# Norm stages of a two-block transformer kernel: token tile 1 starts ahead of tile 0's last held weight, turns and weight splits in a new order

## The reference

```python
def rmsnorm(x, w):
    xf = x.astype(jnp.float32)
    y = xf * lax.rsqrt(jnp.mean(xf * xf, axis=-1, keepdims=True) + RMS_EPS)
    return (y * w.astype(jnp.float32)).astype(x.dtype)

# first block, behind the mixers
x = x + merged @ w_merge_out                       # merge stage, norm with ffn_norm
x = x + (silu(h @ w_gate) * (h @ w_up)) @ w_down   # first feed-forward, norm with norm_mix_w_2
# second block
x = x + nsa_mixer(h, ...)                          # NSA-output stage, norm with norm_cross_w_2
x = x + memory_cross_attention(h, mem_n, ...)      # cross-output stage, norm with norm_ffn_w_2
x = x + conv_ffn(h, ...)                           # second feed-forward, norm with final_norm_w_2
return rmsnorm(x, final_norm_w)
```

## Time and profile before

| | us |
|---|---|
| median of 3 runs | 1783.47 |
| lowest and highest run | 1782.94, 1786.35 |
| profiled execution | 1786.1 |
| its span | 1784.3 |
| TensorE busy in it | 1720.2 (96%) |
| VectorE, ScalarE, GpSimd busy | 955.8, 844.5, 960.9 |

### The profile page before, as it was taken

How to read it: one execution, slowest core, us unless ns; L and a number is a source line. 1 busy time by engine, 2 the same in 40 slices (tenths; PEclk the granted TensorE clock), 3 DMA queues, 4 the chain that set the end, 5 groups by cost and what they waited for, 6 DMA issues and landing times. The chain is left out here.

```text
span 1784.3 us, 27614 instructions
## 1 busy us (share of the span) xinstructions
PE 1720.2 (96%) x10430; PEld 1526.1 (86%) x10430; DVE 955.8 (54%) x1628; ACT 844.5 (47%) x1681; POOL 960.9 (54%) x701
## 2 busy tenths in 40 slices
PE   6999999999999999999989999999899999999998
PEld 4898887888879998999868978888788789989996
DVE  2246564444538851674138469984224388518842
ACT  3234454232336641554336358874434466426642
POOL 2353332334445774776336459982652368648852
PEclk8999999999999999999989999999999999999999
DMA  6332221223342333233325330002442223323331
GB/s 222 93 83 57 72 69 45 60 64 91 117 165 70 97 125 100 78 113 124 89 76 145 109 87 10 14 24 71 135 128 69 67 81 101 118 84 95 118 120 47
DMA packets 222900, 162.09 MB, mean 91 GB/s; under 512 B 9768, under 2 KB 197296, under 8 KB 222768
## 3 DMA queue, kind: packets, MB, share of 16 engines
q1 hardware_dynamic: 221712, 159.26, 29.7%
q10 hardware_dynamic: 1056, 1.06, 0.2%
HBM read 156.09 MB, written 2.11 MB: 89 GB/s over the span
## 5 line engine op out<-in xcount | busy, mean ns | idle before, releaser
L352 POOL TENSOR_TENSOR w_low<-ring,w_high 128x1024 fp32r<-128x1024 f32 (+2 forms) x223 | 484.6, 2177 | 604.4 <-ACT w_high L344 604.0
L365 PE MATMUL psum<-hT,w_high 128*128 128x512 f32 (+1 forms) x1104 | 379.7, 344 | 7.4 <-PEq L184 6.1
L344 ACT ACTIVATE w_high<-ring 128x1024 fp32r<-128x1024 f32 (+2 forms) x223 | 212.3, 955 | 361.1 <-PE psum L367 356.5
L367 PE MATMUL psum<-hT,w_low 128*128 128x512 f32 (+1 forms) x1104 | 373.9, 339 | 0.0
L366 PE MATMUL psum<-hL,w_high 128*128 128x512 f32 (+1 forms) x1104 | 373.9, 339 | 0.0
L365 PEld LDWEIGHTS psum<-hT,w_high 128*128 128x128 f32 x1104 | 210.9, 191 | 28.9 <-issue 7.3
L367 PEld LDWEIGHTS psum<-hT,w_low 128*128 128x128 f32 x1104 | 210.7, 191 | 22.8
L366 PEld LDWEIGHTS psum<-hL,w_high 128*128 128x128 f32 x1104 | 211.0, 191 | 20.0
L1799 POOL TENSOR_TENSOR w_low<-ffn_sums,w_high 128x512 fp32r<-128x512 f32 x120 | 169.8, 1429 | 49.7 <-ACT w_high L1794 49.4
L365 PE MATMUL psum<-ffn_th,w_high 128*128 128x256 f32 x640 | 181.7, 284 | 4.7 <-DVE ffn_g L2047 3.1
L1799 POOL TENSOR_TENSOR w_low<-ring,w_high 128x512 fp32r<-128x512 f32 x120 | 155.7, 1300 | 55.6 <-ACT w_high L1794 49.1
(11 more groups left out here) (441 smaller groups left out, 3760.1 us busy)
## 6 DMA issues: line engine op xcount, KB each, us to landing
ring<-in_w_in SPq DMA_DIRECT2D x58, 512.0 KB, 3.6
ring<-in_ffn_w_up SPq DMA_DIRECT2D x44, 512.0 KB, 3.8
ring<-in_w_gate SPq DMA_DIRECT2D x22, 512.0 KB, 3.8
ring<-in_w_up SPq DMA_DIRECT2D x22, 512.0 KB, 4.9
ring<-in_w_down SPq DMA_DIRECT2D x20, 512.0 KB, 3.9
ring<-in_ffn_w_down SPq DMA_DIRECT2D x20, 512.0 KB, 3.8
ring<-in_nsa_w_in SPq DMA_DIRECT2D x18, 512.0 KB, 3.6
ring<-in_ca_wkv SPq DMA_DIRECT2D x16, 512.0 KB, 3.7
```

Of the source, the lines that this page charges most:

```text
L344: nc.scalar.activation(tile_view(w_high, n, SPLIT), tile_view(ring, n, RING), ACT.Copy).then_inc(w_hi, 1)
L352: nc.gpsimd.tensor_tensor(tile_view(w_low, n, SPLIT), tile_view(ring, n, RING), tile_view(w_high, n, SPLIT), ALU.subtract).then_inc(w_lo, 1)
L365: nc.tensor.matmul(ps, lhsT=sh, rhs=mh, start=first, stop=False)
L367: return nc.tensor.matmul(ps, lhsT=sl, rhs=mh, start=False, stop=last)
```

## The change

On TensorE (`held_tile(t, i)` is held weight i of token tile t) the order of the held part becomes (0,0) (0,1) (1,0) (0,2) (1,1) (1,2), then for token tiles 2 and 3: the first held weight, the turn of the tile two before, the other two held weights; then turn 2 and, with `last_turn`, turn 3. In the key stage turn 3 stands ahead of tile 1. On ScalarE a Sqrt of the constant `eps` into an unused column of `stat` (L679 of the changed kernel) stands ahead of the first chunk's squares, the last held split goes ahead of the memory's high parts, and the next stage's first weights are split ahead of the high parts of tiles 1 and 2, the third one ahead of tile 3's in nsaO alone. The stages with `whole` (merge, cross output) keep their order of splits and high parts.

```diff
+                        def held_tile(t, i):
+                            s = per - held + i
+                            wh, wl = tile_for(pe, n0 + s, wname)
+                            for kk in range(plan[n0 + s][2]):
+                                mm = products(s, kk, wh, wl, t)
+                            if t == tiles - 1:
+                                mm.then_inc(w_used, 1)
+                            elif i == held - 1:
                                 mm.then_inc(tile_done, 1)
-                            if t >= 1 and not store:
-                                if t == 1:
-                                    pe.wait_ge(out_v, tiles)
-                                    if between is not None:
-                                        between["turn"](pe)
-                                norm.turn(pe, t - 1)
-                        if held and not store and last_turn:
-                            norm.turn(pe, tiles - 1)
+
+                        def turn_tile(t):
+                            if store:
+                                return
+                            if t == 0:
+                                pe.wait_ge(out_v, tiles)
+                                if between is not None:
+                                    between["turn"](pe)
+                            norm.turn(pe, t)
+
+                        if held:
+                            held_tile(0, 0)
+                            held_tile(0, 1)
+                            held_tile(1, 0)
+                            held_tile(0, 2)
+                            held_tile(1, 1)
+                            held_tile(1, 2)
+                            for t in range(2, tiles):
+                                held_tile(t, 0)
+                                turn_tile(t - 2)
+                                held_tile(t, 1)
+                                held_tile(t, 2)
+                            turn_tile(tiles - 2)
+                            if last_turn:
+                                turn_tile(tiles - 1)
...
                         split_high(a, n0 + SPLIT)
+                        nc.scalar.activation(stat[:, 151:152], eps, ACT.Sqrt)
                         for t in range(tiles):
                             a.wait_ge(out_v, t + 1)
                             norm.square(a, t, 0, BANK)
+                        split_high(a, n0 + per)
                         if between is not None:
                             between["a"](a)
-                        split_high(a, n0 + per)
                         for t in range(tiles):
                             a.wait_ge(out_v, tiles + t + 1)
                             norm.square(a, t, BANK, BANK)
                             norm.root(a, t)
-                            if whole is not None and t == tiles - 2:
-                                split_high(a, n0 + per - min(SPLIT, per) + SPLIT + 1)
+                            if not store and t >= tiles - 2:
+                                split_high(a, n0 + per - min(SPLIT, per) + SPLIT + 1 + (t == tiles - 1))
                             if t >= 1 and not store:
                                 norm.high_part(a, t - 1)
-                            if t == tiles - 2:
-                                split_high(a, n0 + per - min(SPLIT, per) + SPLIT + (2 if whole is not None else 1))
-                        split_high(a, n0 + per - min(SPLIT, per) + SPLIT + 2)
+                            if whole is not None and t == tiles - 2:
+                                split_high(a, n0 + per - min(SPLIT, per) + SPLIT + 2)
                         if not store:
+                            if not last_turn and whole is None:
+                                split_high(a, n0 + per - min(SPLIT, per) + SPLIT + 3)
                             norm.high_part(a, tiles - 1)
...
         def last_norm_turn(pe, i):
 
-            if i == 2:
+            if i == 1:
                 norm2.turn(pe, NT - 1)
```

More of the change, by code:

```diff
@@ L600, in _ @@
                             between["pe"](pe)
-                        for t in range(tiles if held else 0):
-                            for s in range(per - held, per):
-                                wh, wl = tile_for(pe, n0 + s, wname)
-                                for kk in range(plan[n0 + s][2]):
-                                    mm = products(s, kk, wh, wl, t)
-                                if t == tiles - 1:
-                                    mm.then_inc(w_used, 1)
-                            if t < tiles - 1:
-                                mm.then_inc(tile_done, 1)
-                            if t >= 1 and not store:
-                                if t == 1:
-                                    pe.wait_ge(out_v, tiles)
-                                    if between is not None:
-                                        between["turn"](pe)
-                                norm.turn(pe, t - 1)
```

## The result

The changed kernel takes 1769.91 us (median of 4 runs, 1768.38 to 1771.35), the kernel before, run beside it, 1783.40 (1782.94 to 1786.35): a ratio of 0.9921, with a 95% interval of 0.9904 to 0.9938. That is 13.5 us less; 1769.7 was forecast. The profiled execution after took 1771.35, with a span of 1769.6 us at a mean granted clock of 0.992; before it was 1786.1, 1784.3 and 0.986. The two mean clocks can't be set against one another: from 26.99 to 31.68 the products of 512 columns start 0.43 apart in the profile after, as they do at 1.2 GHz, and 0.23 further on, yet a window from 15 to 35 says 1.00 there; before, where the same stretch is as slow, it says 0.74.

What follows compares the result with a forecast made beforehand. TensorE's waits for w_low, the low weight half GpSimd makes (11.3 us in 8 waits), were taken as the bound a norm-stage change can touch. -1.9 - 1.9 - 10.2 + 0.2 = -13.8, from 1783.5 to 1769.7; range 1765.5 to 1776.

Steps and rivals of the forecast that it cites:

- Merge stage: Merge stage: wait for the third weight's low half gone, next weight split earlier; next stage starts 1.9 us earlier.
- The cover of 1.52 for the added 1.48: Merge stage, ScalarE: early table load (1.28) and root (0.2) hidden by the 1.52 us in which ScalarE waited.
- Cross-output stage: Cross-output stage: same stage and waits as merge, 1.9 us less; the following 1.93 wait for VectorE keeps its size.
- rival (b): Merge and cross-output gains given back at the head of the feed-forward stages; price up to 3.8 us, chance 0.10.
- NSA-output and key stage: NSA-output and key stages: key tile 3 begins 10.2 us earlier, from holes 7.5, restarts and a turn 0.7, clock 2.0.
- the wait left for the first two key weights: Key stage, TensorE: tile 0 without a wait listed, tile 1's weight about 0.5 us late.
- The 2.0 us given for it: Key stage: 22 products at 1.2 GHz took 4.6 us where 2.6 would do; 2.0 of the 10.2.
- the split ahead of the memory parts: NSA-output stage: last held weight split before the memory high parts; alone removes the 1.55 us wait, reordering alone leaves little.
- Feed-forward output stages: Two feed-forward output stages: tile 0 comes 1.36 us later, table load of 1.28 goes; +0.08 each, sum +0.2.
- Rival (a): Clock falls all the same; 1.2 GHz stretches elsewhere may come out longer or shorter; price 2 to 4 us, chance 0.12.
- Rival (c): Key stage keeps most waits, its second and third weight tiles late for another reason; price up to 10 us, chance 0.08.
- (d): Key stage: a late ring tile load holds up normalised tiles and key tile 4; 1784 to 1790 us, chance 0.03.

Runs made afterwards that it cites:

- early-split versions: Two versions of the changed kernel with tile 0's held pieces together in the feed-forward output stages and next-stage weights split earlier: 1772.64 and 1770.88 us.
- last-turn experiment: The kernel before with one edit, the NSA norm's last turn ahead of key tile 1 and not tile 2: 1776.13 us, ratio 0.9951.
- last turn and splits: The kernel before with the last turn ahead of key tile 1 and the changed split order, without held order or early root: 1775.18 us, 0.9941.
- last turn back: The changed kernel with the last turn ahead of key tile 2, as before: 1773.15 us, ratio 0.9927.
- the three loads: The changed kernel with two more table loads beside the early root, ahead of the first chunk's squares: 1775.76 us, ratio 0.9952.
- all next splits earlier: Changed kernel, tile 0 together in feed-forward outputs; second and third next weights split earlier in NSA-output and first feed-forward output stages: 1772.64 us, 0.9927.
- the second key split early: Changed kernel, tile 0 together in feed-forward outputs; in the NSA-output stage the second key weight split ahead of tile 3's square: 1770.88 us, 0.9923.
- the third split in the feed-forward too: Changed kernel, tile 0 together in feed-forward outputs; third weight split ahead of the last high part in the first feed-forward output too: 1766.84 us, 0.9901.

## Why the prediction was right, step by step

The total came out 0.2 from the forecast. Part of that is luck: the stages gave 13.3 where 13.8 was forecast, and the difference between the medians also holds what the clock does elsewhere.

- **Merge stage, 1.9 forecast, 1.83 measured.** The cover of 1.52 for the added 1.48 held to 0.03. The experiment without the root and the one without the held order confirm the two halves: neither half reaches more than 0.6 alone. Turn 0 and turn 1 found their data, and the next stage begins in a wait of 0.22 for the weight instead of 0.2 for tile 1's low part.
- **Cross-output stage, 1.9 forecast, 1.85 measured.** And the wait at the head of the second feed-forward kept its size, 1.93: rival (b) did not come. The reason given, that VectorE's work there runs on from the last low part, holds as far as the size of that wait shows.
- **NSA-output and key stage, 10.2 forecast, 9.66 measured.** The holes went where the steps put them. The term that was off is the wait left for the first two key weights: 0.23 and 0.77, where the text had none and about 0.5, which is 0.5 of the 0.54. GpSimd's subtraction for key tile 0 at 1245.88 was counted at 2.4 and took 2.87 beside VectorE's scaling; the one for tile 1 at 1250.63 began during a scaling too. The forecast named no rival for that, although the trace before had such a meeting (below); it is the same contention that undid the two early-split versions. The clock of 1.00 came as forecast, and the last-turn experiment shows that the low stretch goes with the hole of 4.20. The 2.0 us given for it is not measured apart from the hole.
- **Which edit brings it.** The text said that the split ahead of the memory parts removes the 1.55 by itself and that the reordering alone would leave little. Both hold (no wait, and 0.22). What it did not say is how unequal the edits are: one moved turn alone gives 6.95 of the 9.67 us of its stretch, and the third split, which it told as one of the steps, 0.6 beside it.
- **Feed-forward output stages, +0.2 forecast, +0.07 in the first.** The cost of a later tile 0 and the gain of the moved load do cancel. Keeping them apart, which the forecast did not think of, is worth 1.4 us by the medians and 2.5 by the rows: load early, tile 0 early too.
- **Rival (a), the clock.** It came with the other sign and at the place it named. Seven of the other traces (the held order taken back, last turn and splits, last turn back, the three loads, all next splits earlier, the second key split early, the third split in the feed-forward too) show a slow stretch behind the wait of 1.93 to 1.95 us, the changed kernel and the other five do not. The length of the wait doesn't tell them apart (1.93 to 1.95 with a stretch, 1.93 to 1.94 without). So 1.5 us goes one way or the other in one profile. The medians are of several executions each; how often the stretch comes in them can't be read from their times, and that stays open.
- **Rival (c)** did not come. Of **(d)**, a late load, there is no trace: the splits for the key stage follow ScalarE's own work or TensorE, and none waits for a load.

## What to carry to other kernels

Where an in-order engine makes the next stage's operands, ask what each of its waits depends on, and whether the engine that it waits for will itself wait for what is queued behind: moving one instruction out of such a circle was worth more than all reordering around it. Two edits that each remove a wait may show nothing alone, because each runs into the wait that the other removes; cost them together, and test them apart and together. And before a piece of GpSimd work is moved earlier, look at what VectorE runs at that time.

## What the runs showed of the hardware

**A scaling on VectorE and a subtraction on GpSimd wait for one another, and the one that began first keeps its pace.** A scaling of 128x512 takes 0.75 us by itself. The 14 traces have 34 that met a running subtraction of 128x1024, and all ended 0.54 to 0.56 after that one's end, whether it had 0.8 us left or 2.36. Two of them stand in the kernel before, where the last tile's pair of scalings in the merge stage takes 2.00 and not 1.42:

```profile
546.59 2.00 DVE L439 SCALAR_TENSOR_TENSOR wnorm_h<-x,stat,wnorm_gain 128x512 f32<-128x512 f32 x2
544.98 2.40 POOL L352 TENSOR_TENSOR w_low<-ring,w_high 128x1024 fp32r<-128x1024 f32 x1 [0.50 <-ACT w_high L344]
```

A subtraction takes 2.34 to 2.41 and took 2.83 to 2.88 when it began 0.12 to 0.13 behind the start of a scaling (1245.88 in the changed kernel, 888.16 in the version with the third split in the feed-forward too), which kept its own length. The Trainium skill (GPSIMD Engine Reference, Key points) says that GpSimd shares its SBUF interfaces with VectorE's instructions that have two inputs in SBUF, and the traces agree: both instructions have two. That section gives no price; here it was up to the whole length of the other's instruction. That the earlier one holds the way to SBUF for its whole length is my reading of these rows.

**A table load cost 1.28 us and no drain.** The Trainium skill (ScalarE: Activation LUTs, What ACT_TABLE_LOAD costs) adds 1380 ns; five loads in rows, three of them in turn, are followed at once by the next instruction, and each begins within 0.02 of the end of the one ahead. By the page's figure the version with two more loads would have taken 1781, as its expectation says, and it took 1775.8.

**The clock's fall behind a short wait is not a matter of the wait alone.** A hole of 4.2 us was followed by a stretch at 1.2 GHz in both traces that have it (the kernel before, and the held order alone, whose window 1260 to 1274 shows 0.76), and so were both waits of 2.60 with three loads. Of two waits of about 2.1, the one of 2.04 was followed by such a stretch and the one of 2.10 was not. Behind the same 1.93 to 1.95 at the head of the second feed-forward the clock fell in 8 of 14 profiles. What decides it no run here shows.
